# Retention's off-diagonal tiles and norms split between ScalarE and VectorE, and the fourth retrieval moved between its steps

## The reference

```python
proj = x @ w_in                       # retention q,k,v,gate and attention q,k,v
s = einsum('bhid,bhjd->bhij', qi, ki) * decay_in          # 4 heads, chunks of 128
inner = einsum('bhij,bhjv->bhiv', s, vi)
cross = einsum('bhid,bhdv->bhiv', qi, state) * decay_q
r = silu(rg) * head_norm(r_out)                            # mean and variance over 128
d = head_norm_rms((softmax(q1 k1) - lam * softmax(q2 k2)) @ v) * (1 - lam_init)
x = layer_norm(ALPHA * x + concat(r, d) @ w_out)           # ln1
top_s, top_i = top_k(x @ w_query . sub_keys, 16)           # 8 heads, 2 halves, 128 keys
best_s, pos  = top_k(all 256 sums of two halves, 16)       # experts of a token: 8 x 16
h   = gelu(x . expert_u[idx])                              # 128 experts for each token
x   = layer_norm(ALPHA * x + sum(softmax(best_s) * h * expert_v[idx]))
```

## Time and profile before

| | |
|---|---|
| median of 3 runs | 1594.28 us (1594.04 to 1595.39) |
| profiled execution | 1593.78 us, span 1592.0 us |
| PE, DVE, ACT, POOL busy | 81%, 71%, 17%, 46% of the span |
| weight loads PEld busy | 39% |
| DMA | 603.45 MB, mean 379 GB/s over the span |
| mean granted TensorE clock | 0.92 |

### The profile page before, as it was taken

How to read it: one execution, slowest core, us unless ns; L and a number is a source line. 1 busy time by engine, 2 the same in 40 slices (tenths; PEclk the granted TensorE clock), 3 DMA queues, 4 the chain that set the end, 5 groups by cost and what they waited for, 6 DMA issues and landing times.

```text
span 1592.0 us, 11574 instructions
## 1 busy us (share of the span) xinstructions
PE 1288.4 (81%) x3512; PEld 619.0 (39%) x3512; DVE 1123.6 (71%) x2626; ACT 271.6 (17%) x771; POOL 737.2 (46%) x645
## 2 busy tenths in 40 slices
PE   8999989977678995788787777778787868778787
PEld 5466446433334563333233333333333323333232
DVE  1459999777787967987676768676767686755555
ACT  0200100212122110121212121212121212121111
POOL 0006475767656456454444443535353444344430
PEclk9999989998889998899989898979998899899988
DMA  9859898989889989999999999999999999999994
GB/s 349 352 216 390 296 364 298 412 289 341 286 295 348 351 329 416 381 421 422 421 422 422 421 421 421 422 422 421 421 422 421 421 422 421 422 421 422 421 422 177
DMA packets 100254, 603.45 MB, mean 379 GB/s; under 512 B 11616, under 2 KB 11872, under 8 KB 47584
## 3 DMA queue, kind: packets, MB, share of 16 engines
q0 software_dynamic: 92160, 536.91, 83.7%
q1 hardware_dynamic: 8032, 65.80, 10.3%
HBM read 600.57 MB, written 2.10 MB: 379 GB/s over the span
## 4 chain that ended last, share of the span: by engine, by line
DMA 43%; PE 22%; DVE 21%; POOL 7%; issue 4%; ACT 1%; SPq 1%; DVEq 0%; POOLq 0%
DMA arena<-uv,idx 41%; PE W L542 7%; POOL arena L505 5%; DVE arena L1142 4%; PE ACC L542 4%; PE W L580 3%; PE W L586 3%; PE W L828 2%; DVE arena L1120 2%; DVE xs L1134 2%; DMA arena<-w_in 1%; PE ACC L529 1%; PE X L664 1%; PE X L795 1%; DVE cand L1405 1%
## 5 line engine op out<-in xcount | busy, mean ns | idle before, releaser
L1142 DVE SCALAR_TENSOR_TENSOR arena<-arena,xs 128x1024 f32<-128x1024 f32 x384 | 466.9, 1226 | 293.2 <-DMA arena<-uv,idx 291.4
L489 POOL DMA_INDIRECT arena<-uv,idx x384 | 426.8, 1112 | 530.2 <-PE W L542 310.8
L542 PE MATMUL W<-arena,fdiag 128*128 128x512 f32 x1024 | 494.2, 642 | 144.0 <-ACT fdiag L1072 143.9
L505 POOL DMA_INDIRECT arena<-uv,idx x232 | 282.0, 1216 | 265.3 <-DVE idx L1412 116.9
L542 PEld LDWEIGHTS W<-arena,fdiag 128*128 128x128 f32 x1024 | 206.9, 206 | 430.7 <-issue 249.7
L542 PE MATMUL ACC<-arena,fdiag 128*128 128x512 f32 x512 | 252.8, 655 | 70.4 <-ACT fdiag L1072 70.3
L542 PEld LDWEIGHTS ACC<-arena,fdiag 128*128 128x128 f32 x512 | 105.6, 210 | 217.5 <-issue 131.5
L1072 ACT ACTIVATE fdiag<-ident,gate 128x128 f32<-128x128 f32 x384 | 123.6, 390 | 340.1 <-DVE gate L1150 329.8
L1120 DVE SCALAR_TENSOR_TENSOR arena<-arena,xs 128x1024 f32<-128x1024 f32 x128 | 150.4, 1223 | 22.2 <-DMA arena<-uv,idx 20.8
L580 PE MATMUL W<-arena 128*128 128x512 f32 x272 | 122.7, 605 | 8.7 <-DMA arena<-w_in 8.1
L1134 DVE SCALAR_TENSOR_TENSOR xs<-arena,gate,xs 128x1024 f32<-128x1024 f32 x80 | 102.7, 1284 | 33.4 <-DMA arena<-uv,idx 26.5
(11 more groups left out here) (198 smaller groups left out, 896.6 us busy)
## 6 DMA issues: line engine op xcount, KB each, us to landing
arena<-w_in SPq DMA_DIRECT2D x13, 2048.0 KB, 18.6
arena<-peer_w_query SPq DMA_DIRECT2D x8, 2048.0 KB, 19.8
arena<-uv,idx POOLq DMA_INDIRECT x616, 29.1
arena<-w_out SPq DMA_DIRECT2D x4, 2048.0 KB
arena<-w_in SPq DMA_DIRECT2D x4, 512.0 KB, 6.7
arena<-xT SPq DMA_DIRECT2D x1, 1536.0 KB, 11.8
xs<-x SPq DMA_DIRECT2D x1, 1536.0 KB, 14.6
out<-xs SPq DMA_DIRECT2D x3, 512.0 KB
```

The source lines that it names most:

```text
L489: pool.indirect_dma_start(out=fused[slot], out_offset=None, in_=uv, in_offset=bass.IndirectOffsetOnAxis(ap=idx[:, E + n:E + n + 1], axis=0 ...
L505: pool.indirect_dma_start(out=ring[r], out_offset=None, in_=rows, in_offset=bass.IndirectOffsetOnAxis(ap=idx[:, e:e + 1], axis=0), element ...
L542: last = nc.tensor.matmul(sum_of(b)[:, half * HW:(half + 1) * HW], fdiag[:, n % ND, :], fused[n % NS][:, D + half * HW:D + (half + 1) * HW ...
L1142: STT(out=fused[slot][:, 0:D], in0=fused[slot][:, 0:D], scalar=1.0, in1=xs[:, b, :], op0=ALU.mult, op1=ALU.mult, accum_out=hid[:, E + n:E ...
```

## The change

The decay of a score is written as a factor of the row times a factor of the column. The column factor is a constant over a row of the mixed output, so the norm takes it out if EPS is scaled along with it (`row_eps`). What is left is one number for each partition and head (`across`), and a triangle for the diagonal tile (`near`). So:

- VectorE multiplies the diagonal tiles only. The six others of blocks 1 to 3 are scaled by ScalarE, four passes each, between its copies of the projections.
- The mixes of blocks 1, 2 and 3 go to three banks (X, X, W). VectorE takes only mean and variance of each. Then it makes the inverse roots of all three at once, ScalarE applies them in twelve passes (after its last projection copy), and VectorE does gain, bias and gate for all three in three operations of 1536 numbers.
- `best_pairs` and `best_experts(0, 3)` stand between the retention's steps instead of in heads (1,1), (1,2). The rows are dealt anew: 28 instead of 24 in the retention, 20 instead of 12 in the heads of block 1, none instead of 8 after its norm, five instead of six in a head of block 2, 131 in all by the end of block 2's norm as before.

```diff
-BESIDE_HEAD = {1: 5, 2: 6, 3: 4}
-AFTER_NORM = {1: 8, 2: 3, 3: 11}
+BESIDE_HEAD = {1: 5, 2: 5, 3: 4}
+AFTER_NORM = {1: 0, 2: 3, 3: 11}
...
+        RET_BANKS = [W[:, 3, :], X_BANKS[0], X_BANKS[1], W[:, 3, :]]
...
@@ tensor: retention_mix, attend
-                pe.wait_ge(ret_decayed, tiles_before(b + 1))
-                if b > 1:
-                    pe.wait_ge(ret_normed, b)
+                pe.wait_ge(ret_decayed, b + 1)
+                if b:
+                    pe.wait_ge(ret_scaled, tiles_before(b))
...
                     if b == 1 and h == 0:
-                        pe.wait_ge(ret_normed, NB)
+                        pe.wait_ge(ret_applied, 1)
@@ scalar: project_1
                     take_fill(1, WAVES[1])
+                    for b, jb in OFF_TILES.get(fill[0] - 1 - fill_of(1, RG) - 1, ()):
+                        scale_scores(b, jb)
+                act.wait_ge(ret_scales_ready, 1)
+                for q in range(3):
+                    for h in range(H):
+                        n = q * H + h
+                        last = nc.scalar.activation(ret_out[:, q, h * P:(h + 1) * P], RET_BANKS[q + 1][:, h * P:(h + 1) * P],
+                                                    ACT.Identity, bias=ret_bias[:, n:n + 1], scale=ret_scale[:, n:n + 1])
+                last.then_inc(ret_applied, 1)
+            OFF_TILES = {1: [(1, 0)], 3: [(2, 0), (2, 1)], 6: [(3, 0), (3, 1)], 7: [(3, 2)]}
+            def scale_scores(b, jb):
+                act.wait_ge(ret_scored, tiles_before(b) + jb + 1)
+                act.wait_ge(ret_mixed, b)
+                if b == 1:
+                    act.wait_ge(proj_taken_dve, takes(len(FILLS), "dve"))
+                src = ACC[:, jb % 2 * HW:(jb % 2 + 1) * HW]
+                for h in range(H):
+                    last = nc.scalar.activation(sT[:, jb, h * P:(h + 1) * P], src[:, h * P:(h + 1) * P], ACT.Copy,
+                                                scale=across[:, b - jb - 1, h:h + 1])
+                last.then_inc(ret_scaled, 1)
@@ vector: the three new functions
+            def retention_statistics(b):
+                R = RET_BANKS[b]
+                dve.wait_ge(ret_mixed, b + 1)
+                links([nc.vector.bn_stats(st[:, h, :], R[:, h * P:(h + 1) * P]) for h in range(H)])
+                links([nc.vector.bn_aggr(ret_mv[:, b - 1, h, :], st[:, h, :]) for h in range(H)])
+            def retention_scales():
+                by_block = ret_scale.rearrange("p (q h) -> p q h", q=3)
+                link(TT(out=by_block, in0=ret_mv[:, :, :, 1], in1=row_eps[:].unsqueeze(1).to_broadcast([P, 3, H]), op=ALU.add))
+                inverse_root(ret_scale, 3 * H, ret_root)
+                STT(out=ret_bias.rearrange("p (q h) -> p q h", q=3), in0=ret_mv[:, :, :, 0], scalar=-1.0, in1=by_block,
+                    op0=ALU.mult, op1=ALU.mult).then_inc(ret_scales_ready, 1)
+            def retention_gate():
+                dve.wait_ge(ret_applied, 1)
+                for i, op in ((0, ALU.mult), (1, ALU.add)):
+                    link(TT(out=ret_out, in0=ret_out, in1=gn[:, i, :].unsqueeze(1).to_broadcast([P, 3, HW]), op=op))
+                link(TT(out=swish[:], in0=ret_out, in1=swish[:], op=ALU.mult))
@@ vector: the program
-            for b in range(1, NB):
-                for jb in range(b + 1):
-                    decay_scores(b, jb)
-                    if jb % 2:
-                        rows(HALF)
-                if b > 1:
-                    rows(HALF)
-                retention_norm(b)
-
+            decay_scores(1)
+            rows(HALF)
+            retention_statistics(1)
+            best_pairs()
+            rows(HALF)
+            decay_scores(2)
+            rows(HALF)
+            retention_statistics(2)
+            best_experts(0, 3)
+            rows(HALF)
+            decay_scores(3)
+            rows(2 * HALF)
+            retention_statistics(3)
+            retention_scales()
             weights(0)
+            rows(HALF)
+            retention_gate()
             for b in range(1, NB):
                 for h in range(H):
                     softmax_max(b, h)
                     if b > 1 and h == 2:
                         rows(2)
                         ln1(b - 1)
-                    elif (b, h) == (1, 1):
-                        best_pairs()
-                        rows(1)
-                    elif (b, h) == (1, 2):
-                        best_experts(0, 3)
-                        rows(1)
                     else:
                         rows(BESIDE_HEAD[b])
```

More of the change, by code:

```diff
@@ L216, in build @@
         work = part(3 * K + 3072, D)
-        dec = part(5 * K, D, "p (c n) -> p c n", c=2)
+        near = part(5 * K, HW)
+        across = part(5 * K + HW, 3 * H, "p (o h) -> p o h", o=3)
+        eps_in = part(5 * K + HW + 3 * H, H)
         gn = part(5 * K + D, 1536, "p (i n) -> p i n", i=3)
@@ L1269, in fills_of, with decay_scores, retention_norm_0 @@
                 return [n for n, f in enumerate(FILLS) if f[0] == w and f[1] == g]
[L1271 to L1281, removed]
-                                  scalar=decay_far[h] ** (off - 1), in1=dec[:, 1, h * P:(h + 1) * P],
-                                  op0=ALU.mult, op1=ALU.mult)
-                    ins.then_inc(ret_decayed, 1)
-            def retention_norm(b):
-                R = W[:, 3, :]
-                q = b - (b > 0)
-                dve.wait_ge(ret_mixed, b + 1)
+            def decay_scores(b):
+                dve.wait_ge(ret_scored, tiles_before(b) + b + 1)
+                src = ACC[:, b % 2 * HW:(b % 2 + 1) * HW]
+                TT(out=sT[:, b, :], in0=src, in1=near, op=ALU.mult).then_inc(ret_decayed, 1)
+            def retention_norm_0():
+                R = RET_BANKS[0]
+                dve.wait_ge(ret_mixed, 1)
                 links([nc.vector.bn_stats(st[:, h, :], R[:, h * P:(h + 1) * P]) for h in range(H)])
                 links([nc.vector.bn_aggr(mv[:, h, :], st[:, h, :]) for h in range(H)])
-                link(TS(rstd[:], mv[:, :, 1], EPS, None, ALU.add))
-                inverse_root(rstd[:], H)
+                link(TT(out=rstd[:], in0=mv[:, :, 1], in1=row_eps[:], op=ALU.add))
+                inverse_root(rstd[:], H, root)
                 for h in range(H):
@@ L1544, in constants @@
     i = np.arange(P)
-    rel = (i[None, :] - i[:, None])[:, None, :]
-    near = np.where(rel >= 0, np.exp(np.maximum(rel, 0) * log_g[None, :, None]), 0.0)
-    far = np.exp((rel + P) * log_g[None, :, None])
-    decay = (np.stack([near, far], axis=1) * P ** -0.5).reshape(P, 2, HW)
+    left = np.exp((P - 1 - i)[:, None] * log_g[None, :]) * P ** -0.5
+    near = (i[None, None, :] >= i[:, None, None]) * left[:, :, None]
+    across = left[:, None, :] * np.exp(P * np.arange(1, NB)[None, :, None] * log_g[None, None, :])
+    row_eps = EPS * np.exp(2.0 * (P - 1 - i)[:, None] * log_g[None, :])
+    decay = np.concatenate([near.reshape(P, -1), across.reshape(P, -1), row_eps], axis=1)
     ang = np.arange(S)[:, None] * (10000.0 ** (-np.arange(64) / 64.0))[None, :]
@@ L1582 @@
     out = nc.dram_tensor("out", (S, D), fp32, kind="ExternalOutput").ap()
[L1583 removed]
+    build(nc, *aps, out)
     r = run_bass_kernel_spmd(nc, [arrays], core_ids=[0])
```

48 lines of the change are left out of this document (29 added, 19 removed).

## The result

The changed kernel takes 1598.15 us, the median of 14 runs (1594.65 to 1602.42); the kernel before, in turn with it on the same chip, 1594.44 (14 runs). The ratio is 1.0028, 95% interval 1.0017 to 1.0039: slower by 0.28%, 3.7 us. The time lies in the range that was forecast, on the wrong side of no change.

The account below looks back on a forecast made before the run. DMA-bound from 561.5 us, so only block 1's first gather start counts. Shifts: 9.2 late at the first head, 2.4 at U24, 1.5 at dot 112, then 2.5 early: 1591.3 profiled, 1591.8 median, range 1585 to 1600.

Parts of the forecast that it names:

- first maximum: Start of head (1,0)'s maxima on VectorE, behind the gate: forecast 9.2 us late, near 308 instead of 299.22.
- the 7 us wait at 405.43: GpSimd's 7.17 us wait for a VectorE dot in block 2's heads, before the change; forecast to go.
- V1's last slot is free at 333.6 ... V2's last slot at 348.3: Heads (1,1) and (1,2): when TensorE frees the slots GpSimd needs for the last rows of V3 and V4.
- U24 starts at 349.7: GpSimd's row-gather quad U24 during block 1's heads: forecast 2.4 us late, against 347.29 before.
- GpSimd issues without a stop: From U24 on GpSimd catches up, lag 1.5 us at U28, so dot 112 starts at 392.2 for 390.65.
- the next hold is U31, which wants dot 116: Block 2's heads: GpSimd's next hold, forecast at 413.2 instead of 417.13, 3.9 us early at U31's first row.
- 2.5 early from 445.77 to the end: From block 2's row wait on, everything shifts alike; taken as 2.5 us, between 1.5 and 3.9.
- 5.5 us early instead of the 10.0: Block 1's heads: U22 starts at 321.8 against 327.25, less than the 10.0 us the two removed waits cost.
- lead is kept: Rival: the 5.5 us lead at U22 survives to U24 and adds to block 2's gain, 8 us, 1586; chance 0.23.
- The late gate is paid: Rival in block 1's three heads: slower row landing counts three times before U24, 1599 to 1606; chance 0.22.
- Swallowed: Rival: GpSimd's quads or TensorE's rows are tight between 405 and 561, shifts end within 1 us, 1594; chance 0.10.
- two waits of 10.0 us: GpSimd's waits at U22 for slots not freed by VectorE's dots, 7.33 and 2.71 us; forecast to go.

Follow-up runs that it names:

- a1_again: The changed kernel run once more, unaltered, for a second profile: 1598.26 us, ratio 1.0028 to the kernel before.
- c2: The changed kernel with ScalarE's passes before its last projection copy but one and the gate before weights(0), still five dots per block 1 head: 1598.09 us, ratio 1.0024.
- c1: The changed kernel with passes before the last projection copy but one, gate before weights(0), three dots per block 1 head, eight behind its norm: 1579.30 us, ratio 0.9905.
- a3: The changed kernel with three dots per block 1 head and eight behind its norm, instead of five and none: 1586.72 us, ratio 0.9950.
- b2: The kernel before with only the join and look-up moved and the rows dealt as in the changed kernel, retention as before: 1604.55 us, ratio 1.0070.
- d1: The kernel before with join and look-up moved, old retention, three dots per block 1 head and eight behind its norm: 1585.61 us, ratio 0.9951.
- b1: The changed kernel's new retention alone, with join, look-up and dealing of rows as in the kernel before: 1600.66 us, ratio 1.0049.
- c3: New retention alone, join, look-up and dealing as before, with passes before the last projection copy but one and gate before weights(0): 1591.83 us, ratio 0.9987.
- a2: The changed kernel with ScalarE's twelve passes ahead of its copy of the last projection instead of behind it: 1595.51 us, ratio 1.0005.
- a4_clock: The changed kernel with extra unread products filling TensorE's waits in the heads of block 1: 1595.87 us, ratio 1.0011, interval 0.9997 to 1.0026.

## Why the prediction was wrong

**What held.** TensorE ends the retention, and VectorE's shorter sum bought nothing by itself. Twelve passes take 4.28 us (4.7 forecast), and the gate 5.3 (5.4). No table load stands before the passes; the one behind them, for Exp, took 1.28 us. The Trainium skill ("ScalarE: Activation LUTs", Table sets) has identity in every set, and the trace agrees. So the first maximum was 8.6 us late (9.2 forecast), 6.4 in `a1_again`. The early look-up gave nothing. The 24 scalings lay hidden. U22 started at 322.32 (321.8), the waits before dots came in (1,1), (1,2), (1,3), and the 7 us wait at 405.43 went. The last 1030 us only moved.

**The step that failed** is "V1's last slot is free at 333.6 ... V2's last slot at 348.3", from which "U24 starts at 349.7". U24 started at 354.50, 7.2 us later than before and not 2.4. The terms: the join of (1,1) ended 1.15 late (U22 0.5, landing 6.5 instead of 6). From its end to V3's last issue were 4.1 us and not 2.2, 1.9 more, and the same again in (1,2), 4.4 for 2.4. The 2.2 lets the fourth row run at 1.88 us, as in head (1,0), where TensorE had been busy. It comes after an idle 5.4 to 6.1 us, and there it took 3.31 and 3.62, with the transposes 0.69 instead of 0.38. 1.15 + 1.9 + 2.0 is 5.05; the rest of the turn was 0.25 shorter than forecast, and 4.8 was missed. The working had the idle TensorE in it and never asked at what clock it would go on. In `a1_again` the miss was smaller, U24 at 352.02, 2.3 late. The landmarks behind carry the miss on: U31 was 4.8 late against its forecast of 413.2, and 2.3 in `a1_again`; the first gather, forecast near 559, came at 563.03 and 564.34. So the profiled execution is 3.4 us over the 1591.3 of the sum, and the median, 1598.15, 6.3 over its 1591.8.

**A wrong reading behind it**, worth about 1 us of these 4.8, is in block 2. By "GpSimd issues without a stop" landed rows were to pace dot 112, at 392.2, and "the next hold is U31, which wants dot 116", 413.2. Landed rows paced neither. VectorE had no dots left to do behind block 1's norm and stood 6.52 us for TensorE's score of head (2,0). Dot 112 started at 396.27 and dot 116 at 415.58, both without a wait:

```profile
382.46 0.43 DVE L1359 TENSOR_TENSOR W<-W,mask 128x256 f32<-128x256 f32 x1 [6.52 <-PE W L753]
...
396.27 1.22 DVE L1160 SCALAR_TENSOR_TENSOR arena<-arena,xs 128x1024 f32<-128x1024 f32 x1
...
415.58 1.22 DVE L1160 SCALAR_TENSOR_TENSOR arena<-arena,xs 128x1024 f32<-128x1024 f32 x1
```

Dot 116 ended at 416.80, so the hold that the forecast priced would have let U31 go at about 417. Another came with it, which the forecast didn't have, V7: its four issues waited for TensorE's V5 rows (2.84, 0.78, 0.78 and 2.71 us, the last at 416.73), and U31 started at 417.97, 0.8 late instead of 3.9 early. The eight dots that had stood behind block 1's norm now stood ahead of it, so TensorE came to the heads of block 2 later. The addition of the first three V5 rows, beside head (2,2), began at 407.40, 15 us later than before. Two rows of TensorE before, which the forecast hadn't read:

```profile
392.23 5.42 PE L529 MATMUL ACC<-arena,fdiag 128*128 128x512 f32 x12
...
403.23 3.62 PE L529 MATMUL ACC<-arena,fdiag 128*128 128x512 f32 x4
```

With them 413.2 would have been read as a lower bound only. By both, "2.5 early from 445.77 to the end" became 2.1 late at 447.86 and 1.5 late at the first gather (2.8 in `a1_again`).

**What the lead was.** "5.5 us early instead of the 10.0" compared U22's first issue with its last. Row by row V3's first was at 327.28 for 329.24, 2.0 early. The sum didn't add the 5.5, but the rival "lead is kept" did, and with it got a chance that it hadn't earned. It did name one thing rightly: with VectorE standing, most issues from 322.32 to 368 take 0.94 us. That gave nothing, since GpSimd then waited for slots.

**The rivals.** "The late gate is paid" had the sign, the place and the multiplier (three heads, each at the pace of its data). Its cause was wrong. Landing was 6.5, 5.4 and 5.3 us (322.32 to 328.83, 337.91 to 343.27, 354.50 to 359.83), 5.7 in the mean where I took 6. What was longer was TensorE's part of the ring. Its name was wrong too: c2 puts the gate on time and stays at 1598.1. "Swallowed" was partly right, by the mechanism it named, quads tight elsewhere: of c1's 16.9 us lead at U31 14.2 reach the first gather, of a3's 8.0 6.3.

**The cause, as shown.** Three pairs differ in the dealing alone: after and a3 (1598.2, 1586.7), c2 and c1 (1598.1, 1579.3), b2 and d1 (1604.6, 1585.6). Five dots per head of block 1, in place of three and eight behind the norm, cost 11.4, 18.8 and 18.9 us. The greater part of each is there at U24 already (9.3, 15.0 and 16.4 us), ahead of the dots behind the norm. Moving the gate to its time gives 8.8 in the dealing of before (b1, c3), 7.4 with three dots (a3, c1) and nothing with five (after, c2), though about half of the way there gave 2.75 (a1_again, a2). The new retention was worth 6.3 us with three dots and an early gate (d1, c1), and nothing with a late one (d1, a3: 1585.6, 1586.7). The forecast weighed the move as two waits of 10.0 us that go, and the five dots as the same work elsewhere. It should have asked of each dot in a head whether its row is issued before that head begins.

**Left open.** How much of the 3.7 us is TensorE's clock: `a4_clock` lifts only part of it and its interval is wide. Why c2 is slower than a2, beyond GpSimd's longer issues. Why `a1_again` is 1.7 us early at U31 and 2.8 late at the first gather is half known: one piece is the chance of the clock below, the rest isn't traced.

## What to carry to other kernels

A list that says how many pieces of work stand in each step is a schedule of the slots that they free. Before raising such a number, follow one piece round: which transfer it needs, who issues that, which slot the issuer waits for, and who frees it; if the way comes back to the same step, the step takes the sum of the way whatever is sped up beside it. Read an engine that is about to be idle at the clock that it will then have. New work behind a last copy stands in the way of all that the copy releases; here two places further up in ScalarE's queue were worth 7 to 9 us with the ring open, and with the ring closed one place gave 2.75 us and two gave nothing.

## What the runs showed of the hardware

A row product of four 512-wide fp32 matmuls took 1.88 us on a busy TensorE, and 3.1 to 3.6 after an idle stretch of 4.9 (before, 402.54) to 8.5 us (after, 367.12); the window's mean granted clock fell from 0.89 to 0.81, so parts ran at the lower of its two levels, 1.2 GHz. After an idle 3.0 us both come about, in the same head (3,2) and with the same program. TensorE of after, then of `a1_again`:

```profile
477.33 0.66 PE L776 MATMUL W<-ident,arena 128*128 128x128 f32 x4 [3.04 <-DVE arena L1371]
477.83 1.88 PE L542 MATMUL ACC<-rv,fdiag 128*128 128x512 f32 x4
```

```profile
477.16 1.11 PE L776 MATMUL W<-ident,arena 128*128 128x128 f32 x4 [2.97 <-DVE arena L1371]
478.07 2.94 PE L542 MATMUL ACC<-rv,fdiag 128*128 128x512 f32 x4
```

The product is 1.1 us longer and the transposes 0.45, 1.5 in one place of one execution. Before, `a3_three_dots` and `c3_retention_on_time` took 1.88 at this place too, after an idle 2.96, and `a2_apply_early` 3.62 after 3.03. The Trainium skill ("TensorE: Matmul & The Clock Gate", What's actually happening) calls the number of products at the low clock run-variable, and these rows agree. Single executions of the changed kernel lie up to 3.5 us under and 4.3 over their median, and a single profile can't tell a change of this size.

A 128-wide pass of ScalarE out of a bank with both scale and bias from memory took 0.36 us in a row (4.28 for twelve), one with the scale alone 0.27 (eight in 2.17).
